# Value matmuls of B and C at full width with the denominators inside, and a limit on the projections per step

## The chip, the cores and the metric

The program runs on all 8 NeuronCores of one Trainium2 chip, one batch element each, with the same instructions on every core. The metric is the device time of the slowest core in microseconds. TensorE (PE in the profile) multiplies, ScalarE (ACT) computes exponentials and other functions, VectorE (DVE) combines and copies, GpSimd (POOL) and SyncE (SP) mainly start transfers. Each engine works through its own queue in order and waits on semaphores.

## The reference

Two layers; in each a mixer with three attentions in parallel and a SwiGLU network. D_MODEL is 1024, a core has 2048 frames. The part that the change touches are the attentions B and C, 8 heads of width 64 each:

```python
def forgetting_attention(q, k, v, f_logit):            # B: causal per frame
    ...
    sc = jnp.einsum('bqhd,bshd->bhqs', qb, k).astype(jnp.float32) * scale
    sc = sc + cq[..., :, None] - cum[:, :, None, :]
    sc = jnp.where(kpos[None, :] <= qpos[:, None], sc, NEG_INF)
    p = jax.nn.softmax(sc, axis=-1)
    return jnp.einsum('bhqs,bshd->bqhd', p.astype(v.dtype), v)

def chunked_relpos_attention(q, k, v, rel_table):      # C: own chunk and 8 before it
    ...
    sc = jnp.einsum('bqhd,bshd->bhqs', qc, kc).astype(jnp.float32) * scale + bias
    sc = jnp.where(valid[None, None, None, :], sc, NEG_INF)
    p = jax.nn.softmax(sc, axis=-1)
    return jnp.einsum('bhqs,bshd->bqhd', p.astype(vc.dtype), vc)
```

The kernel computes the softmax without a maximum: exponentials of the scores, their product with V, their sum over the keys (a product with ones), and a division at the end.

## The kernel before

`Prog` records operations per engine and derives the semaphore waits; each engine's queue is the order in which the Python code emits. Everything is feature-major: a tile of scores has 128 keys on the partitions and up to 512 queries (a group g, four of them) in the columns.

**Stages of a layer.** Attention A (31 steps), then four pairs of heads of B (36 steps each), four of C (18 each), then the merge of the branches, the output projection and the FFN. `seq` at the end of `build` lists the pairs; the two sets of buffers QK[s], VB[s] alternate.

**A step** (`run_steps`, L590) works on one pair of heads and one or two key tiles: the score matmuls of both heads into two banks, one exponential of ScalarE over both (PTF), then *filler*, and then, one step late, `emit_pv` (L558) with the value matmuls of the step before. Filler are the projections of the next pair, of which `pair_filler` (L767) hands out two matmuls at a time. `want` (L611) spreads them evenly over the steps: total is 96 per pair (106 in B of layer 0, with blocks of the conditioning). A projection unit has 8 matmuls of 512 columns (`proj_fm`) or 32 of 128 columns (`proj_v`) and ends with VectorE's evacuation of the one bank AJ; then a yield of 0 ends the filler of that step, and one of -1 (Q and K of a B pair) also skips the next step.

**Values and denominators.** `emit_pv` issues for each key tile and head a matmul with 64 columns of V, and one with 64 columns of ones, to partitions 0 to 63 or 64 to 127 of the banks `ob` (4 and 5 in turn) and DB (6). So both heads lie in one accumulator, and their denominators in another. `fin_pair` (L510) ends a group: Ln of the denominators in the same step, Exp of its negative in the next, the product by VectorE into OT in the one after; `run_pend` runs these stages.

Of the kernel before, what the change touches and what calls it, by code (L numbers as in the profile page):

```python
# [6 lines left out]
F32 = mybir.dt.float32  # L7
# [10 lines left out]
GS = 512  # L18
# [215 lines left out]
def build(order=None, nl=DEPTH):  # L234
# [33 lines left out]
    def sb(name, shape, dt):  # L268
        return nc.alloc_sbuf_tensor("sb_" + name, list(shape), dt)

    XR = sb("XT", [128, NG * 4096], F32)
    HT = sb("HT", [128, NCH, S], BF16)
    RR = sb("W", [128, 22528], BF16)
    NS = 6
    WS = sb("WS", [128, NS, 2048], BF16)
    RS = sb("RS", [128, 2, GS], F32)
    PT = sb("PT", [128, 8, GS], BF16)
    TMPF = sb("TMPF", [128, 3, GS], F32)
    RD = sb("RD", [128, 2, GS], F32)
# [216 lines left out]

    def proj_v(wv3, wb, t4, VB, vbufs, bi):
        for q in range(4):
            t = t4 * 4 + q
            pe_group([(PS[bi][:, q * 128:(q + 1) * 128], HT[:, kc, tl(t)], wv3[:, kc, :], kc == 0, kc == 7) for kc in range(8)],  # L500
                     [wb] + [ht[kc][t4] for kc in range(8)], [psb[bi]])
            if q < 3:
                yield 2
        copy("dve", VB[:, t4 * 512:(t4 + 1) * 512], PS[bi][:, :], [psb[bi]], [vbufs[t4]])

    def drain(gen):
        for _ in gen:
# [23 lines left out]
            tt(out, i0, i1, ALU.mult, [psb[ob], rdb[ri]], wr)  # L531
        return [st0, st1, st2]

    SETO = [0, 10240]
    QK = [[RR[:, o + i * 2048:o + (i + 1) * 2048] for i in range(4)] for o in SETO]
    VB = [RR[:, o + 8192:o + 10240] for o in SETO]
    qb = [[[Buf() for _ in range(NG)] for _ in range(4)] for _ in range(2)]
    augb = [[Buf() for _ in range(4)] for _ in range(2)]
    vbb = [[Buf() for _ in range(4)] for _ in range(2)]
    setbufs = [flat(qb[s]) + augb[s] + vbb[s] for s in range(2)]  # L540
    AO = 10240
    QA = RR[:, AO:AO + 8192].rearrange("p (c t) -> p c t", c=4)
    KA = RR[:, AO + 8192:AO + 10240]
    VA = RR[:, AO + 10240:AO + 12288]
# [7 lines left out]

    AJ = 7
    DB = 6
    HS = [slice(0, 64), slice(64, 128)]
    pipe = {"held": None, "pend": []}

    def emit_pv():  # L558
        if pipe["held"] is None:
            return  # L560
        st, pp, ptr = pipe["held"]
        pipe["held"] = None
        bi = st["ob"]
# [23 lines left out]
        while pipe["pend"]:  # L587
            run_pend()

    def run_steps(steps, filler, total):  # L590
        n = len(steps)
        given = 0
        cool = -1
        for i in range(n):
# [13 lines left out]
            if i == 0:  # L608
                emit_pv()
            if filler is not None and i > cool:  # L610
                want = total * (i + 1) / n  # L611
                while given < want:
                    c = next(filler, None)
                    if c is None:
                        filler = None
                        break
                    if c <= 0:
                        cool = i - c
                        break
                    given += c  # L620
# [161 lines left out]
    def pair_steps(l, is_b, s, p):  # L782
        k_out = 1 if is_b else 2
        steps = []
        for g in range(NG):
            ob = ob_alloc()
            started = []

            def fin(ob=ob, g=g):
                return fin_pair(ob, OT[k_out][:, p, sl(g)], [ot[k_out][p][g]])  # L790

            def add(kts, last=False):
                qk, bias, pv, pr = [], [], [], [onesbuf]
                qr = [cb] + ([qb[s][0][g], qb[s][1][g]] + augb[s] if is_b else [qb[s][0][g], biascb[s]])
                off = 0
                for j in kts:
# [13 lines left out]
                    else:  # L810
# [7 lines left out]
                            rows = HS[hh]  # L818
                            qk.append((hh, off, off + w, QK[s][2][rows, tl(j)], QK[s][0][rows, qs]))
                        qr.append(qb[s][2][j // 4])  # L820
                    pv.append((off, c0, c0 + w, VB[s][:, tl(j)], not started))
                    started.append(j)
                    pr.append(vbb[s][j // 4])
                    off += w
# [160 lines left out]
    for l in range(nl):  # L985
        a_rest(l)
        run_steps(a_steps(l), a_filler(l), 128)
        seq = [(True, p) for p in range(4)] + [(False, p) for p in range(4)]
        for i, (is_b, p) in enumerate(seq):
            run_steps(pair_steps(l, is_b, i % 2, p), pair_filler(l, i, seq) if i < 7 else None, 96 + (10 if l == 0 and i < 4 else 0))  # L990
        flush_pipe()
        wos = merge(l, x_d if l == 0 else xs_d)
        prev = None
# [151 lines left out]
```

How the kernel before makes its waits and increments, by code:

```python
        def run(e, engobj):  # L163
            for o in self.ops[e]:
                for ev in o.deps:
                    if ev.kind == "eng":
                        engobj.wait_ge(sems[ev.eng], ev.op.count)
                    else:
                        engobj.wait_ge(ev.sem, ev.value)
                inst = o.fn(engobj)
                if o.is_dma:
                    inst.then_inc(o.dma_sem, 16)
                elif o.needed:
                    inst.then_inc(sems[e], 1)
            if e == "sp":
                for b in final_waits:
                    ev = b.last_write
                    if ev is None:
                        continue
                    if ev.kind == "dma":
                        engobj.wait_ge(ev.sem, ev.value)
                    else:
                        engobj.wait_ge(sems[ev.eng], ev.op.count)
```

## Time and profile before

| what | value |
|---|---|
| median of 3 runs | 2815.0 us (2814.04 to 2816.72) |
| profiled execution | 2812.6 us, span 2810.8 us, 43124 instructions |
| cores in it | 2805.0 to 2810.8 us, granted TensorE clock 0.980 to 0.983 |
| TensorE busy | 2654.0 us (94%), 16192 matmuls |
| ScalarE, VectorE, GpSimd busy | 989.2 (35%), 983.3 (35%), 250.9 us (9%) |
| TensorE waits for ScalarE's probabilities (sb_PT) | 7.5 us, 25 times |
| TensorE waits for VectorE's sb_RD (A's denominators) | 43.8 us, 16 times |

In layer 0 of this execution the first pair of B begins at 252 us, C at 504.5, the merge at 663.2; in layer 1 at 1615, 1864.4 and 2023. In a timeline row the first number is the start in us from the start of the span and the second the duration of the row; "x8" stands for eight instructions of one form merged into one row; "128*64" is the number of rows and columns of the weights. A matmul's duration overlaps the next one's, so distances are taken from start to start. Score matmuls read sb_W,sb_W ("ps<-sb_W"), value matmuls sb_PT,sb_W, the ones sb_PT,sb_onesb, projections sb_HT and sb_WS.

### The profile page before, as it was taken

Reading aid. Unit: us, or ns where it says so; the run is one execution under the profiler, and the core shown is the slowest. Engines: PE = TensorE matmul, PEld = TensorE weight load, DVE = VectorE, ACT = ScalarE, POOL = GpSimd, SP = SyncE. Lnnn points to the kernel's source line nnn. Section 1 sums busy time; section 2 is a strip of 40 time slices with the busy share of each in tenths; the row PEclk is TensorE's granted clock in tenths of the full one; section 3 lists DMA queues with packets and bytes.
Section 4 is the critical chain, followed back from the end, with each engine's and each line's share of the span. In section 5 each row is a group of like instructions: output and inputs, shape, how many; then the busy total and the mean of one; then the engine's idle time right before and its main releaser. Section 6 shows DMA issues by size and latency. Waiting matters only on the chain.

```text
span 2810.8 us, 43124 instructions; the slowest of 8 cores (2805.0 to 2810.8 us)
## 1 busy us (share of the span) xinstructions
PE 2654.0 (94%) x16192; PEld 1203.2 (43%) x16192; DVE 983.3 (35%) x1471; ACT 989.2 (35%) x1334; POOL 250.9 (9%) x318
## 2 busy tenths in 40 slices
PE   1779999999999999999989799999999999999998
PEld 0323444554444444444433244445544444444443
DVE  1543222222444522223254522222244453232326
ACT  1355666544222421110144466654522234101012
POOL 2001000000000210000130010000000021000002
PEclk9889999999999999999999899999999999999999
DMA  9112222211223453343341010112122343222213
GB/s 214 16 27 41 47 47 35 53 30 24 35 34 48 118 92 68 53 77 59 68 136 23 9 18 17 20 20 55 18 34 40 51 113 53 38 38 38 45 31 120
DMA packets 68889, 147.83 MB, mean 53 GB/s; under 512 B 9504, under 2 KB 21920, under 8 KB 66640
## 3 DMA queue, kind: packets, MB, share of 16 engines
q0 software_dynamic: 55712, 99.66, 22.5%
q1 hardware_dynamic: 12976, 45.41, 4.8%
q8 instruction: 135, 2.21, 0.3%
q14 instruction: 66, 0.54, 0.1%
HBM read 227.53 MB, written 16.78 MB: 87 GB/s over the span
## 4 chain that ended last, share of the span: by engine, by line
PE 90%; DVE 3%; DMA 2%; ACT 2%; issue 2%; DVEq 0%; POOL 0%; POOLq 0%; ACTq 0%
PE ps L375 71%; PE ps L373 19%; DMA sb_WS<-wada 2%; ACT sb_PT L385 1%; ACT sb_HT L385 1%; DVE sb_XT L394 0%; DVE sb_RD L389 0%; DMA sb_WS<-win 0%; DVE sb_TMPF L394 0%; DVE sb_W L404 0%; DVE sb_XT L695 0%; DVE sb_W L398 0%; ACT sb_TMPF L385 0%; DMA sb_WS<-wfi 0%; DVE sb_XT L404 0%
## 5 line engine op out<-in xcount | busy, mean ns | idle before, releaser
L375 PE MATMUL ps<-sb_HT,sb_WS 128*128 128x512 bf16 (+1 forms) x5760 | 1342.9, 385 | 38.4 <-ACT sb_HT L385 22.4
L375 PEld LDWEIGHTS ps<-sb_HT,sb_WS 128*128 128x128 bf16 (+1 forms) x5760 | 556.4, 99 | 736.2 <-issue 108.3
L385 ACT ACTIVATE sb_PT<-ps 128x1024 bf16<-128x1024 f32 (+1 forms) x494 | 488.6, 989 | 430.8 <-PE ps L373 426.7
L385 ACT ACTIVATE sb_TMPF<-ps 128x512 f32<-128x512 f32 x388 | 231.3, 597 | 1141.6 <-PE ps L375 1141.4
L375 PE MATMUL ps<-sb_W,sb_WS 128*128 128x512 bf16 x1920 | 417.9, 379 | 1.2 <-DVE sb_W L389 1.1
L389 DVE TENSOR_TENSOR sb_W<-ps,sb_TMPF 128x512 bf16<-128x512 f32 x176 | 121.3, 691 | 484.5 <-PE ps L375 472.5
L375 PEld LDWEIGHTS ps<-sb_W,sb_WS 128*128 128x128 bf16 x1920 | 187.5, 98 | 227.2 <-issue 2.1
L404 DVE CAST sb_W<-ps 128x512 bf16<-128x512 f32 (+1 forms) x176 | 121.5, 690 | 408.5 <-PE ps L375 407.9
L373 PE MATMUL ps<-sb_W 128*128 128x512 bf16 (+7 forms) x1212 | 257.9, 340 | 0.0
L394 DVE SCALAR_TENSOR_TENSOR sb_XT<-ps,sb_modT,sb_XT 128x512 f32<-128x512 f32 x256 | 186.3, 748 | 154.2 <-PE ps L375 154.1
L373 PE MATMUL ps<-sb_PT,sb_onesb 128*64 128x512 bf16 (+3 forms) x1212 | 188.6, 336 | 44.4 <-DVE sb_RD L389 43.8
L373 PE MATMUL ps<-sb_PT,sb_W 128*64 128x512 bf16 (+3 forms) x1212 | 197.5, 352 | 8.9 <-ACT sb_PT L385 7.5
L375 PE MATMUL ps<-sb_XT,sb_WS 128*128 128x512 bf16 x768 | 197.1, 379 | 0.0
L389 DVE TENSOR_TENSOR sb_PT<-ps,sb_TMPF 128x512 f32<-128x512 f32 x128 | 88.5, 692 | 190.9 <-PE ps L375 184.7
L398 DVE TENSOR_SCALAR sb_W<-ps 128x512 bf16<-128x512 f32 (+1 forms) x128 | 88.0, 689 | 178.9 <-PE ps L375 178.1
L375 PE MATMUL ps<-sb_WS,sb_HT 128*128 128x128 bf16 x2304 | 144.0, 219 | 0.0
L375 PEld LDWEIGHTS ps<-sb_WS,sb_HT 128*128 128x128 bf16 x2304 | 132.8, 98 | 17.9 <-issue 8.3
L373 PEld LDWEIGHTS ps<-sb_W 128*128 128x128 bf16 (+1 forms) x1212 | 67.8, 95 | 158.5 <-issue 138.9
L389 DVE TENSOR_TENSOR sb_XT<-ps,sb_RD 128x512 bf16<-128x512 f32 x96 | 66.2, 689 | 182.6 <-ACT sb_RD L385 182.5
L373 PEld LDWEIGHTS ps<-sb_PT,sb_W 128*64 128x64 bf16 x1212 | 59.4, 107 | 164.6 <-issue 154.0
L375 PEld LDWEIGHTS ps<-sb_XT,sb_WS 128*128 128x128 bf16 x768 | 75.1, 98 | 90.6
L394 DVE SCALAR_TENSOR_TENSOR sb_TMPF<-sb_XT,sb_gsc,sb_RS 128x512 f32<-128x512 f32 x128 | 86.3, 745 | 47.5 <-ACT sb_RS L385 47.4
(53 smaller groups left out, 1187.7 us busy)
## 6 DMA issues: line engine op xcount, KB each, us to landing
sb_WS<-wada POOLq DMA_DIRECT2D x48, 512.0 KB, 9.3
sb_WS<-wfi POOLq DMA_DIRECT2D x44, 512.0 KB, 6.4
sb_WS<-wmg POOLq DMA_DIRECT2D x48, 384.0 KB, 5.7
sb_XT<-x SPq DMA_DIRECT2D x8, 2048.0 KB, 16.2
sb_WS<-win POOLq DMA_DIRECT2D x60, 256.0 KB, 4.3
sb_WS<-wfo POOLq DMA_DIRECT2D x24, 512.0 KB, 6.3
xs<-sb_XT SPq DMA_DIRECT2D x4, 2048.0 KB, 6.3
sb_XT<-xs SPq DMA_DIRECT2D x4, 2048.0 KB, 17.1
```

The lines of the kernel that those rows point to most:

```text
L373: r = e.matmul(o, lhsT=l, rhs=rr, start=st, stop=sp, skip_group_check=True)
L375: r = e.matmul(o, lhsT=l, rhs=rr, start=st, stop=sp)
L385: return P.op("act", lambda e, o=out, i=in_, f=func, kw=kw: e.activation(out=o, in_=i, func=f, **kw), reads=reads, writes=writes)
L389: return P.op(eng, lambda e, o=out, a=in0, b=in1, op=op: e.tensor_tensor(out=o, in0=a, in1=b, op=op), reads=reads, writes=writes)
L394: e.scalar_tensor_tensor(out=o, in0=a, scalar=s_, in1=b, op0=p0, op1=p1),
L398: return P.op(eng, lambda e, o=out, a=in0, s1=s1, p0=op0: e.tensor_scalar(out=o, in0=a, scalar1=s1, scalar2=None, op0=p0), reads=reads, wr ...
L404: return P.op(eng, lambda e, o=out, i=in_: e.tensor_copy(out=o, in_=i), reads=reads, writes=writes)
```

## The change

Each V tile gets 192 columns instead of 128: V of the even head, 64 ones, V of the odd head. A value matmul takes 128 of these as weights, so one matmul per key tile and head computes values and denominators, on opposite halves of one bank per head. Three banks (4, 6, 5) serve two accumulators per group in rotation. At a group's end `fin_two` first copies both banks to SBUF, then computes Ln per head across the halves, one Exp, and two half products. The ones are set once per set of buffers by GpSimd; the casts of V write in two pieces of 64 columns. `want` is two matmuls ahead of before and also limited per step: 6 (layer 0) or 4 (layer 1) in B, 8 in C, none in A. What is left is issued after the last step of a pair. A keeps `fin_pair`. The lines of after.py behind the change are two or more higher than before's.

```diff
-    RR = sb("W", [128, 22528], BF16)
+    RR = sb("W", [128, 23552], BF16)
+    OS = sb("OS", [128, 2, GS], F32)
...
-        copy("dve", VB[:, t4 * 512:(t4 + 1) * 512], PS[bi][:, :], [psb[bi]], [vbufs[t4]])
+        if len(VB.shape) == 2:
+            copy("dve", VB[:, t4 * 512:(t4 + 1) * 512], PS[bi][:, :], [psb[bi]], [vbufs[t4]])
+        else:
+            dst = VB[:, t4 * 4:t4 * 4 + 4, :].rearrange("p t (a c) -> p t a c", c=64)[:, :, 0:3:2, :]
+            copy("dve", dst, PS[bi][:, :].rearrange("p (t a c) -> p t a c", t=4, a=2), [psb[bi]], [vbufs[t4]])
...
+    def fin_two(ob, out, wr):
+        ri = next_rot("rd", 2)
+        def st0():
+            for hh in range(2):
+                copy("dve", OS[:, hh, :], PS[ob[hh]][:, :], [psb[ob[hh]]], [osb[hh]])
+        def st1():
+            for hh in range(2):
+                act(RD[HS[hh], ri, :], OS[HS[1 - hh], hh, :], AF.Ln, [osb[hh]], [rdb[ri]])
+            act(RD[:, ri, :], RD[:, ri, :], AF.Exp, [], [rdb[ri]], scale=-1.0)
+        def st2():
+            for hh in range(2):
+                tt(out[HS[hh], :], OS[HS[hh], hh, :], RD[HS[hh], ri, :], ALU.mult, [osb[hh], rdb[ri]], wr)
+        return [st0, st1, st2]
...
+    OB3 = [4, 6, 5]
...
+        if isinstance(bi, list):
+            for hh in range(2):
+                pe_group([(PS[bi[hh]][:, a:b], v[:, hh * 64:hh * 64 + 128],
+                           PTF[:, pp * 1024 + hh * GS + off:pp * 1024 + hh * GS + off + b - a], first, False, True)
+                          for (off, a, b, v, first) in st["pv"]], ptr + st["pr"], [psb[bi[hh]]])
+            if st["fin"] is not None:
+                f = st["fin"]()
+                f[0]()
+                pipe["pend"].append([f[1], f[2]])
+            return
...
-                want = total * (i + 1) / n
+                want = min(total * (i + 1) / n + 2, given + cap)
...
+            memset(VB[s][:, :, 64:128], 1.0, [vonb[s]] + vbb[s])
...
-            ob = ob_alloc()
+            ob = [OB3[next_rot("ob3", 3)], OB3[next_rot("ob3", 3)]]
...
-            run_steps(pair_steps(l, is_b, i % 2, p), pair_filler(l, i, seq) if i < 7 else None, 96 + (10 if l == 0 and i < 4 else 0))
+            run_steps(pair_steps(l, is_b, i % 2, p), pair_filler(l, i, seq) if i < 7 else None, 96 + (10 if l == 0 and i < 4 else 0), (6 if l == 0 else 4) if is_b else 8)
```

TensorE's queue in the first B pair of layer 1, from the first score matmuls (ps<-sb_W) of the third group, before:

```order
L373 MATMUL ps<-sb_W 128x512 x2
L373 MATMUL ps<-sb_PT,sb_W 64x256 x2
L373 MATMUL ps<-sb_PT,sb_onesb 64x256 x2
L373 MATMUL ps<-sb_W 128x512 x2
L375 MATMUL ps<-sb_HT,sb_WS 128x512 x8
L373 MATMUL ps<-sb_PT,sb_W 64x512 x2
L373 MATMUL ps<-sb_PT,sb_onesb 64x512 x2
L373 MATMUL ps<-sb_W 128x512 x2
L373 MATMUL ps<-sb_PT,sb_W 64x512 x2
L373 MATMUL ps<-sb_PT,sb_onesb 64x512 x2
```

and in the changed kernel:

```order
L375 MATMUL ps<-sb_W 128x512 x2
L375 MATMUL ps<-sb_PT,sb_W 128x256 x2
L375 MATMUL ps<-sb_W 128x512 x2
L375 MATMUL ps<-sb_PT,sb_W 128x512 x2
L375 MATMUL ps<-sb_W 128x512 x2
L377 MATMUL ps<-sb_HT,sb_WS 128x512 x4
L375 MATMUL ps<-sb_PT,sb_W 128x512 x2
L375 MATMUL ps<-sb_W 128x512 x2
L377 MATMUL ps<-sb_HT,sb_WS 128x512 x4
L375 MATMUL ps<-sb_PT,sb_W 128x512 x2
```

The matmuls with ones are gone, the value matmuls have 128 weight columns, and a unit of projections lies in two steps instead of one, followed by two steps without any (before too there were two without).

TensorE's queue at the end of the first C pair of layer 0, before:

```order
L373 MATMUL ps<-sb_W 128x512 x2
L375 MATMUL ps<-sb_WS,sb_HT 128x128 x32
L373 MATMUL ps<-sb_PT,sb_W 64x128 x2
L373 MATMUL ps<-sb_PT,sb_W 64x384 x2
L373 MATMUL ps<-sb_PT,sb_onesb 64x128 x2
L373 MATMUL ps<-sb_PT,sb_onesb 64x384 x2
L373 MATMUL ps<-sb_BIASC,sb_identb 128x256 x2
```

and in the changed kernel:

```order
L375 MATMUL ps<-sb_W 128x512 x2
L375 MATMUL ps<-sb_PT,sb_W 128x128
L375 MATMUL ps<-sb_PT,sb_W 128x384
L375 MATMUL ps<-sb_PT,sb_W 128x128
L375 MATMUL ps<-sb_PT,sb_W 128x384
L377 MATMUL ps<-sb_WS,sb_HT 128x128 x96
L375 MATMUL ps<-sb_BIASC,sb_identb 128x256 x2
```

Three units of V's projection (96 matmuls of 128 columns) now stand together between the last step of this pair and the first scores of the next (sb_BIASC is C's bias).

VectorE's queue in layer 0 while the second C pair runs, before (sb_XT<-ps,sb_RD is a group's final product; the casts and TENSOR_SCALAR to sb_W are evacuations of projections):

```order
L398 TENSOR_SCALAR sb_W<-ps 128x512
L389 TENSOR_TENSOR sb_XT<-ps,sb_RD 128x512
L398 TENSOR_SCALAR sb_W<-ps 128x512 x2
L389 TENSOR_TENSOR sb_XT<-ps,sb_RD 128x512
L398 TENSOR_SCALAR sb_W<-ps 128x512
L404 CAST sb_W<-ps 128x512 x2
```

and in the changed kernel:

```order
L400 TENSOR_SCALAR sb_W<-ps 128x512
L391 TENSOR_TENSOR sb_XT<-sb_OS,sb_RD 64x512 x2
L400 TENSOR_SCALAR sb_W<-ps 128x512
L406 COPY sb_OS<-ps 128x512 x2
L400 TENSOR_SCALAR sb_W<-ps 128x512
L391 TENSOR_TENSOR sb_XT<-sb_OS,sb_RD 64x512 x2
```

A group costs VectorE two copies and two half products instead of one product, and evacuations stand between them.

## Rows read from the trace of the kernel before

**Rows 1.** The page, section 4: shares by engine of the chain that ended last.
```profile
PE 90%; DVE 3%; DMA 2%; ACT 2%; issue 2%; DVEq 0%; POOL 0%; POOLq 0%; ACTq 0%
```

**Rows 2.** Windows: B, merge of layer 0; busy us (count) by engine, clock, DMA.
```profile
273.00:505.00 232.00, 230.56 (x1927) 104.37 (x1926) 57.02 (x90) 141.40 (x160) 14.30 (x24) 1.00 0.27 43
...
663.00:972.00 309.00, 309.00 (x1434) 139.99 (x1432) 149.03 (x216) 89.68 (x145) 31.70 (x39) 1.00 0.28 54
```

**Rows 3.** Groups by form: count, busy us, mean ns, idle before; three groups.
```profile
L385 ACT ACTIVATE sb_PT<-ps 128x1024 bf16<-128x1024 f32 x454 | 464.8, 1024 | 406.2 <-PE ps L373 402.5 <-ACT sb_PT L385 0.7
...
L385 ACT ACTIVATE sb_PT<-ps 128x512 bf16<-128x512 f32 x40 | 23.8, 596 | 24.5 <-PE ps L373 24.2
...
L407 POOL MEMSET sb_W<- 128x2048 bf16 x16 | 28.2, 1819 | 37.5 <-PE ps L373 37.5
```

**Rows 4.** Timeline, B of layer 0: start, us, engine, line, operation, idle before.
```profile
422.30 0.60 PE L373 MATMUL ps<-sb_W 128*128 128x512 bf16 x2
...
422.84 0.41 PE L373 MATMUL ps<-sb_PT,sb_W 128*64 128x512 bf16 x2
...
423.00 2.17 ACT L385 ACTIVATE sb_PT<-ps 128x1024 bf16<-128x1024 f32 x2 [1.79 <-PE ps L373]
423.08 0.38 PE L373 MATMUL ps<-sb_PT,sb_onesb 128*64 128x512 bf16 x2
...
423.39 0.60 PE L373 MATMUL ps<-sb_W 128*128 128x512 bf16 x2
...
424.17 0.41 PE L373 MATMUL ps<-sb_PT,sb_W 128*64 128x512 bf16 x2 [0.17 <-ACT sb_PT L385]
```

**Rows 5.** Timeline, B of layer 0, TensorE with eight projection matmuls.
```profile
419.49 0.60 PE L373 MATMUL ps<-sb_W 128*128 128x512 bf16 x2
...
419.93 1.89 PE L375 MATMUL ps<-sb_HT,sb_WS 128*128 128x512 bf16 x8
...
421.75 0.41 PE L373 MATMUL ps<-sb_PT,sb_W 128*64 128x512 bf16 x2
```

**Rows 6.** Chain of waits: the same place in successive B pairs, layers 0 and 1.
```profile
309.87 2.52 PE ps L373 x20
373.01 2.52 PE ps L373 x20
...
1646.23 2.52 PE ps L373 x20
...
1709.07 2.52 PE ps L373 x20
```

**Rows 7.** Timeline, C of layer 0, TensorE: scores, then projections or values.
```profile
590.51 0.39 PE L373 MATMUL ps<-sb_W 64*128 64x512 bf16 x2
...
590.83 1.96 PE L375 MATMUL ps<-sb_WS,sb_HT 128*128 128x128 bf16 x32
...
654.21 0.39 PE L373 MATMUL ps<-sb_W 64*128 64x512 bf16 x2
...
654.53 0.41 PE L373 MATMUL ps<-sb_PT,sb_W 128*64 128x128 bf16 x4
```

**Rows 8.** Timeline, last C pair of layer 0, ScalarE.
```profile
650.67 1.02 ACT L385 ACTIVATE sb_PT<-ps 128x1024 bf16<-128x1024 f32 x1
...
657.41 1.02 ACT L385 ACTIVATE sb_PT<-ps 128x1024 bf16<-128x1024 f32 x1
...
658.33 0.62 ACT L385 ACTIVATE sb_RD<-sb_RD 128x512 f32<-128x512 f32 x1
...
658.89 1.02 ACT L385 ACTIVATE sb_PT<-ps 128x1024 bf16<-128x1024 f32 x1
```

**Rows 9.** Timeline, B of layer 0: a unit of value projections and its cast.
```profile
425.17 1.95 PE L375 MATMUL ps<-sb_WS,sb_HT 128*128 128x128 bf16 x32
...
427.05 0.41 PE L373 MATMUL ps<-sb_PT,sb_W 128*64 128x512 bf16 x2
...
427.23 0.69 DVE L404 CAST sb_W<-ps 128x512 bf16<-128x512 f32 x1 [3.91 <-PE ps L375]
```

More of the change, by code:

```diff
@@ L325, in build @@
     rdb = [Buf() for _ in range(2)]
+    osb = [Buf() for _ in range(2)]
     a8b = Buf()
@@ L532, in fin_pair @@
         return [st0, st1, st2]
-    SETO = [0, 10240]
+    def fin_two(ob, out, wr):
[11 more added lines that the diff above has]
+        return [st0, st1, st2]
+    SETO = [0, 11264]
     QK = [[RR[:, o + i * 2048:o + (i + 1) * 2048] for i in range(4)] for o in SETO]
-    VB = [RR[:, o + 8192:o + 10240] for o in SETO]
+    VB = [RR[:, o + 8192:o + 11264].rearrange("p (t c) -> p t c", t=16) for o in SETO]
     qb = [[[Buf() for _ in range(NG)] for _ in range(4)] for _ in range(2)]
@@ L539, in build @@
     vbb = [[Buf() for _ in range(4)] for _ in range(2)]
-    setbufs = [flat(qb[s]) + augb[s] + vbb[s] for s in range(2)]
-    AO = 10240
+    vonb = [Buf() for _ in range(2)]
+    setbufs = [flat(qb[s]) + augb[s] + vbb[s] + [vonb[s]] for s in range(2)]
+    AO = 11264
     QA = RR[:, AO:AO + 8192].rearrange("p (c t) -> p c t", c=4)
@@ L588, in flush_pipe, with run_steps @@
             run_pend()
-    def run_steps(steps, filler, total):
+    def run_steps(steps, filler, total, cap=99):
         n = len(steps)
@@ L785, in pair_steps @@
         for g in range(NG):
-            ob = ob_alloc()
+            ob = [OB3[next_rot("ob3", 3)], OB3[next_rot("ob3", 3)]]
             started = []
             def fin(ob=ob, g=g):
-                return fin_pair(ob, OT[k_out][:, p, sl(g)], [ot[k_out][p][g]])
+                return fin_two(ob, OT[k_out][:, p, sl(g)], [ot[k_out][p][g]])
             def add(kts, last=False):
-                qk, bias, pv, pr = [], [], [], [onesbuf]
+                qk, bias, pv, pr = [], [], [], [vonb[s]]
                 qr = [cb] + ([qb[s][0][g], qb[s][1][g]] + augb[s] if is_b else [qb[s][0][g], biascb[s]])
@@ L820, in add @@
                         qr.append(qb[s][2][j // 4])
-                    pv.append((off, c0, c0 + w, VB[s][:, tl(j)], not started))
+                    pv.append((off, c0, c0 + w, VB[s][:, j, :], not started))
                     started.append(j)
@@ L987, in build @@
         run_steps(a_steps(l), a_filler(l), 128)
+        state["ob3"] = 0
         seq = [(True, p) for p in range(4)] + [(False, p) for p in range(4)]
         for i, (is_b, p) in enumerate(seq):
-            run_steps(pair_steps(l, is_b, i % 2, p), pair_filler(l, i, seq) if i < 7 else None, 96 + (10 if l == 0 and i < 4 else 0))
+            run_steps(pair_steps(l, is_b, i % 2, p), pair_filler(l, i, seq) if i < 7 else None, 96 + (10 if l == 0 and i < 4 else 0), (6 if l == 0 else 4) if is_b else 8)
         flush_pipe()
```

## The prediction

> **What bounds the kernel now.** I read the chain of waits first, then the stages, then single steps in the timeline. The chain is 90% TensorE [rows 1]: what counts is what TensorE's queue needs, plus the places where it waits. By stages [rows 2], the pairs of B of layer 0 (273 to 505 us) keep it busy over 99% at a granted clock of 1.00; ScalarE is at 61%, VectorE at a quarter. C and layer 1 have the same shape. The exponentials over a score tile count the steps [rows 3]: 454 + 40 = 494, of which A has 31 per layer, so B has 8 x 36 = 288 and C 8 x 18 = 144. A "busy" TensorE hides bubbles, though, since a matmul row is longer than its slot. So I take start-to-start distances. The merge is dense: 309.0 us for 1434 matmuls, 0.2155 us each [rows 2]; I call 0.216 one unit.
>
> A B step without projections [rows 4]: scores at 422.30, values at 422.84, ones at 423.08, next scores at 423.39. That is 1.09 us for four units (two score matmuls, two pairs of half-width ones side by side), 0.864. The excess sits at the borders: scores to values 0.54 instead of 0.43, values to ones 0.24 instead of 0.216, ones to scores 0.31 instead of 0.216. Scores to projections costs nothing (419.49 to 419.93, 0.44), but eight projection matmuls to values take 1.82 instead of 1.73 [rows 5]. So entering and leaving the half-width form costs about 0.10 each, and a step pays 0.225 with or without projections. Check: a B pair of layer 1 takes 62.8 us (1646.23 to 1709.07), one of layer 0 63.1 [rows 6]; the layer 1 pair has 240 units = 51.8 us, and 36 x 0.225 = 8.1, which leaves 2.9 for waits.
>
> The waits: after two steps without projections the value matmuls come 1.87 us after their scores (422.30 to 424.17) and not 1.63, 0.24 late, on the exponential that began at 423.00 [rows 4]. The chain scores, exponential, values is thus 0.70 + 1.02 + 0.15 us. Counted in the order: 8 such places in each of the first three B pairs of layer 1 and 5 in those of layer 0, 39 in all.
>
> **The change, part by part.**
>
> *Value matmuls.* Each key tile and head issued a half-width value and a half-width ones matmul, two heads side by side: two slots per key tile. Now it is one full-width matmul per head: also two slots. The arithmetic gains nothing; the borders go. B: 288 x 0.225 = 64.8 us. In C the scores themselves are in a form of 64 rows, which keeps its border: 590.51 to 590.83 is 0.32 for one unit, both to projections and to values (654.21 to 654.53) [rows 7]. A filled C pair pays 12 x 0.32 + 6 x 0.22 = 5.2 now and 18 x 0.10 = 1.8 afterwards: 3.4, times 6 = 20.2. The last C pair of a layer has no projections: 36 x 0.12 = 4.3. The 39 waits of 0.24 = 9.4 are replaced, not kept (next term). Removed: 98.7.
>
> Whether full-width weights hide behind a running matmul is the point where the Trainium skill and the rows part, in the two sentences that follow. "TensorE: Matmul & The Clock Gate", Part 3, The mechanism, says that a weight load overlaps running matmuls only when its row group differs, which for full-width matmuls would never be so. By that rule each new value matmul would pay its load as well; the merge, whose matmuls are all full-width, speaks against it [rows 2]: 140.0 us of weight loads lie inside 309.0 us of matmuls at 0.2155 each.
>
> *Steps with less cover.* TensorE's step falls to 0.864 without projections, but the chain of 1.87 stays. Two empty steps in a row: 1.30 against 1.87, 0.57 late; the new order has 1 such place in each of the first three B pairs of layer 0 and 8 in those of layer 1, 27 in all: 15.4 us. One empty step beside one with two matmuls: 1.73, 0.14 late, 26 places in layer 0: 3.6. I take 4 off, since some coincide with group ends.
>
> *Group ends.* There are 64, four in each of 16 pairs. Before, ScalarE did one Ln and one Exp in separate steps; now two Ln on 64 rows and one Exp in one block. Back to back in the last pair an exponential occupies 0.92, the Exp on the denominators 0.56, and I take 0.56 for each Ln [rows 8]. From the end of the scores of the group's second step: 0.27 + 0.92 + 3 x 0.56 + 1.02 + 0.15 = 4.04 until the next step's values may start. TensorE's own work there is eight units plus eight projection matmuls, 3.45. Late: 0.59. VectorE: two copies of the accumulators (0.69 each, as the cast of rows 9) free the banks. The second value matmul of the new group needs the first copy: the old group's last matmul of that bank streams 0.11, the copy starts 0.27 later and takes 0.69, 0.15 until TensorE: 1.22 us, against 0.86 of TensorE's work in between without projections (0.11 + 0.11 + 0.43 + 0.216): 0.36 late. This lies inside the window above, so I take 0.6 for both, 32 in B: 19.2. Bounds: 0 (always projections between) and 2.0 (copies behind an evacuation of 2 x 0.69). In C, steps carry eight matmuls or none: 0 to 0.5, taken 0.2, 24 groups of filled pairs: 4.8. VectorE's four operations of 0.69 instead of one add 132 us to 983; it has the room on average.
>
> *Pacing.* The limit per step, together with the skip after each unit, leaves work over: in the new order 96 and 80 matmuls of 128 columns stand at the end of 6 C pairs and of 3 B pairs of layer 1. They use one bank, so each unit of 32 waits for the cast of the one before: matmuls at 425.17, free at 426.96 (0.056 each), cast at 427.23 for 0.69 [rows 9], plus 0.15: 1.11 us. Two per place, 18: 20.0. Bounds 0.9 and 1.4 each. The projections themselves are the same in number.
>
> *The rest.* The last C pair of each layer is bound by ScalarE nearly as much as by TensorE: five steps take 6.7 us (650.67 to 657.41) [rows 8], and its five exponentials, two Ln and Exp come to 5 x 0.92 + 1.68 = 6.3 before dependences. I let the 4.3 removed there vanish; bounds 0 and 8. The fifth memset lies on GpSimd behind four of 1.82 [rows 3] and ahead of loads wanted much later: 0, at most 2. A has its matmuls and its waits in nearly the same places: 0, at most 3 either way. Merge and FFN don't change.
>
> Added: 15.4 + 3.6 - 4 + 19.2 + 4.8 + 20.0 + 4.3 = 63.3. Net -35.4. The profiled execution took 2812.6 us (span 2810.8), so 2777.2; the median of the runs is 2.4 above it: 2780.
>
> **Rivals.** (1) TensorE keeps its cover: group ends and empty steps cost nothing, only the drains: -98.7 + 20.0, 2736 us. For it: the fillers lie at half of the group ends, and TensorE runs dense. Against: the 0.24 is there already today. (2) ScalarE's chain rules: the waits are twice what I take (15.4 + 3.6 - 4 + 19.2 + 4.8 = 39 us more), 2819. For it: in layer 1 the steps' TensorE work falls to 47.5 us per pair (51.8 less the 20 units at the end) against 41.8 of ScalarE (32 x 1.02 + 4 x 0.60 [rows 3] + 4 x 1.68). Against: where a step has projections the chain has room. (3) Slower: VectorE as bottleneck of the bank rotation. With three banks for two accumulators, a copy that stands behind an evacuation (1.39) or behind the multiplications that wait for ScalarE's Exp stops TensorE at every group. With 1.1 more at 56 groups, 62 us more: 2842. It decides from 0.63 us more per group. For it: VectorE gets 2.8 us per group of which group 0 has only three steps. Against: the copies stand ahead of the multiplications of their group, and casts stand mostly two steps away. (4) The change doesn't do what it says: the border is not of the half-width form but of the wait for the probabilities; then 89 us don't go, 2869. Against it: ones to scores has no new wait for an exponential and pays the same 0.10. (5) Weight loads of 1088 full-width value matmuls come into the open, 0.098 each (140.0 / 1432) [rows 2]: +107, 2887. The sentence of the Trainium skill above would say so; the row says no.
>
> **How the numbers follow.** Forecast 0.58 (2760 to 2800), rival 1 0.17 (down to 2730), rival 2 0.15 (2800 to 2825, of which 0.08 still faster and 0.04 no change), rival 3 0.06, rival 4 0.03, rival 5 0.01. A measurement of this kernel can tell about 0.2%, 6 us. Faster 0.83, same 0.04, slower 0.13. Range: 2746 to 2815, half of rival 1 and the slow cases outside.
>
> **What would show it.** In the new profile: in B values start 0.43 after the scores and the next scores 0.43 after the values. B pairs near 59 us in layer 0 and near 62 in layer 1, of that about 2 in the drain; filled C pairs near 43.5, the last unchanged at 25. Waits of TensorE on ScalarE's probabilities rise from 7.5 us to some 40, and waits on VectorE appear once per group. Wrong if the borders of 0.10 are still there, if a wait on the accumulator copies exceeds 1 us on average, or if A, merge or FFN move by over 3 us.

## The result, and the profile after

The changed kernel took 2832.9 us (median of 5; 2829.3 to 2833.3 without disturbance) against 2816.7 for the kernel before: ratio of the undisturbed runs 1.0054, 95% interval 1.0036 to 1.0071. It is slower by half a per cent, where 2780 was forecast. The profiled execution took 2833.3 us, its span 2831.2.

The chain of waits of the changed kernel, by engine (share of the span):

```profile
PE 81%; ACT 6%; DVE 5%; issue 5%; DMA 2%; DVEq 0%; ACTq 0%; POOL 0%; POOLq 0%
```

TensorE's part fell from 90% to 81% [rows 1], ScalarE's and VectorE's rose from 5 to 11. That fits a shorter queue of TensorE with more waits in between; shares of a chain alone don't prove it, the rows below do. The windows of layer 0 of the changed kernel (us, then busy us by engine, granted clock, DMA) stand for B, three filled C pairs, and the last C pair:

```profile
254.00:509.00 255.00, 228.80 (x1760) 124.23 (x1790) 93.22 (x146) 166.02 (x193) 25.57 (x34) 0.97 0.29 45
509.00:643.00 134.00, 122.26 (x1078) 72.37 (x1088) 58.19 (x89) 75.62 (x91) 5.15 (x8) 1.00 0.21 43
643.00:675.00 32.00, 23.66 (x188) 12.46 (x187) 12.42 (x19) 25.05 (x31) 0.71 (x1) 0.90 0.09 14
```

B before kept TensorE busy 99% of its time at clock 1.00 [rows 2]; now it is 90%, at a mean of 0.97. What TensorE waits for in the whole changed kernel (total us, times, longest; L375 are scores and values, L377 projections; its waits for weight transfers and norms, such as 54.3 us for the conditioning's weights, were 50.5 before and are left out):

```profile
PE ps L375 <- DVE sb_RD L391: 43.1, 15, 4.6
PE ps L375 <- ACT sb_PT L387: 39.7, 60, 1.9
PE ps L377 <- DVE sb_W L406: 25.4, 36, 1.1
...
PE ps L377 <- DVE sb_modT L391: 9.5, 5, 2.9
...
PE ps L377 <- DVE sb_W L400: 6.4, 8, 1.0
PE ps L375 <- DVE sb_OS L406: 6.0, 6, 1.5
```

The first row is phase A, as before. The second was 7.5 us. The casts of projections (sb_W) and the add of the conditioning vector (sb_modT) were 1.4 us before and are 41 us together now. Now the timeline of B, layer 0, first at a place where TensorE doesn't wait, then at the end of a group:

```profile
410.05 0.59 PE L375 MATMUL ps<-sb_W 128*128 128x512 bf16 x2
410.48 0.59 PE L377 MATMUL ps<-sb_HT,sb_WS 128*128 128x512 bf16 x2
410.91 0.59 PE L375 MATMUL ps<-sb_PT,sb_W 128*128 128x512 bf16 x2
411.34 0.59 PE L375 MATMUL ps<-sb_W 128*128 128x512 bf16 x2
...
423.19 1.35 ACT L387 ACTIVATE sb_RD<-sb_OS 64x512 f32<-64x512 f32 x2
...
424.01 0.59 PE L377 MATMUL ps<-sb_HT,sb_WS 128*128 128x512 bf16 x2
...
424.63 0.63 ACT L387 ACTIVATE sb_RD<-sb_RD 128x512 f32<-128x512 f32 x1
425.17 1.92 ACT L387 ACTIVATE sb_PT<-ps 128x1024 bf16<-128x1024 f32 x2
425.36 1.48 DVE L391 TENSOR_TENSOR sb_XT<-sb_OS,sb_RD 64x512 bf16<-64x512 f32 x2 [2.34 <-ACT sb_RD L387]
426.32 0.59 PE L375 MATMUL ps<-sb_PT,sb_W 128*128 128x512 bf16 x2 [0.85 <-ACT sb_PT L387]
426.87 1.39 DVE L406 CAST sb_W<-ps 64x512 bf16<-64x512 f32 x2
428.41 1.46 PE L377 MATMUL ps<-sb_HT,sb_WS 128*128 128x512 bf16 x6 [1.07 <-DVE sb_W L406]
```

The first four rows: 0.43 from each to the next, so the borders of 0.10 around the half-width form [rows 4, 5] are gone, as forecast. The others show the group end: two Ln and an Exp occupy ScalarE from 423.19 to 425.17, and the values wait 0.85 for the exponential behind them. VectorE stands 2.34 us before the products, which need that Exp. The cast behind them had its data since the unit of projections ended at 424.60, comes after 1.48 us of products at 426.87, and bank 7 is free for projections only at 428.41: 1.07 more. The second wait was in no term of my sum.

Pair times, from first scores to the next pair's first scores (last C pair: to the merge's first matmul), profiled executions:

| us | before | changed | forecast |
|---|---|---|---|
| A, layers 0 / 1 | 109.4 / 106.4 | 109.4 / 109.3 | same |
| B layer 0, pairs 1 and 2 | 63.2 | 65.2 | 59 |
| B layer 1, pairs 0 to 2 | 62.9 | 62.2, 63.4, 63.2 | 62 |
| filled C pair | 44.4 | 45.0 | 43.5 |
| last C pair | 25.5 | 31.8 | 25.5 |

The fourth pair of B, whose projections are those of C, went from 62.6 to 61.4 in layer 0 and from 60.3 to 56.2 in layer 1. The table compares the slowest core of each execution. Most rows agree within 0.5 us on all eight cores; the second 65.2 is 63.7 on four of them, and the last C pair of layer 1 takes 31.8 to 33.8. A differs most: in layer 1 it takes 106.2 to 109.5 us on the cores of the kernel before and 106.2 to 109.3 on those of the changed one, so the 2.9 in the table is a difference between two cores and not the work of the change.

### The profile page after: what moved, and what is told of

It reads as the page before. It is cut to its first block, busy times and chain, and to the rows that moved or that the text cites. A ratio compares the mean times of both kernels' runs of the same rounds, so it can differ in the third digit from the quotient of the medians.

```text
span 2831.2 us, 41471 instructions; the slowest of 8 cores (2822.7 to 2831.2 us)
## 1 busy us (share of the span) xinstructions
PE 2592.6 (92%) x15104; PEld 1235.4 (44%) x15104; DVE 1109.2 (39%) x1663; ACT 1035.8 (37%) x1398; POOL 254.4 (9%) x322
## 4 chain that ended last, share of the span: by engine, by line
PE 81%; ACT 6%; DVE 5%; issue 5%; DMA 2%; DVEq 0%; ACTq 0%; POOL 0%; POOLq 0%
PE ps L377 69%; PE ps L375 13%; ACT sb_RD L387 2%; ACT sb_PT L387 2%; DMA sb_WS<-wada 2%; DVE sb_W L406 1%; DVE sb_OS L406 1%; ACT sb_HT L387 1%; DVE sb_XT L391 1%; DVE sb_XT L396 0%; DVE sb_TMPF L396 0%; DMA sb_WS<-win 0%; DVE sb_W L400 0%; DVE sb_RD L391 0%; DVE sb_XT L730 0%
## 5 line engine op out<-in xcount | busy, mean ns | idle before, releaser
L377 PE MATMUL ps<-sb_HT,sb_WS 128*128 128x512 bf16 (+1 forms) x5760 | 1353.3, 387 | 62.0 <-ACT sb_HT L387 22.4
L377 PEld LDWEIGHTS ps<-sb_HT,sb_WS 128*128 128x128 bf16 (+1 forms) x5760 | 558.4, 99 | 769.3 <-issue 144.5
L387 ACT ACTIVATE sb_PT<-ps 128x1024 bf16<-128x1024 f32 (+1 forms) x494 | 480.0, 986 | 401.6 <-PE ps L375 395.6
L377 PE MATMUL ps<-sb_W,sb_WS 128*128 128x512 bf16 x1920 | 418.0, 379 | 0.8 <-DVE sb_W L391 0.7
L375 PE MATMUL ps<-sb_PT,sb_W 128*128 128x512 bf16 (+4 forms) x1212 | 281.5, 340 | 46.9 <-ACT sb_PT L387 37.7
L377 PEld LDWEIGHTS ps<-sb_W,sb_WS 128*128 128x128 bf16 x1920 | 187.5, 98 | 226.8 <-issue 1.8
L375 PE MATMUL ps<-sb_W 128*128 128x512 bf16 (+7 forms) x1212 | 256.8, 340 | 0.0
L406 DVE CAST sb_W<-ps 128x512 bf16<-128x512 f32 (+1 forms) x176 | 121.5, 690 | 329.3 <-PE ps L377 311.5
L377 PE MATMUL ps<-sb_XT,sb_WS 128*128 128x512 bf16 x768 | 197.0, 379 | 0.0
L375 PEld LDWEIGHTS ps<-sb_PT,sb_W 128*128 128x128 bf16 (+1 forms) x1212 | 96.1, 99 | 175.3 <-issue 125.3
L377 PE MATMUL ps<-sb_WS,sb_HT 128*128 128x128 bf16 x2304 | 144.4, 219 | 18.3 <-DVE sb_W L406 17.7
L377 PEld LDWEIGHTS ps<-sb_WS,sb_HT 128*128 128x128 bf16 x2304 | 132.2, 98 | 36.4 <-issue 29.8
L391 DVE TENSOR_TENSOR sb_XT<-sb_OS,sb_RD 64x512 bf16<-64x512 f32 x128 | 87.9, 686 | 122.3 <-ACT sb_RD L387 114.8
L400 DVE TENSOR_SCALAR sb_W<-ps 128x512 bf16<-128x512 f32 (+1 forms) x128 | 87.9, 689 | 118.1 <-PE ps L377 109.4
L375 PEld LDWEIGHTS ps<-sb_W 128*128 128x128 bf16 (+1 forms) x1212 | 83.0, 96 | 103.5 <-issue 40.3
L377 PEld LDWEIGHTS ps<-sb_XT,sb_WS 128*128 128x128 bf16 x768 | 75.3, 98 | 91.2 <-issue 1.0
L406 DVE COPY sb_OS<-ps 128x512 f32<-128x512 f32 x128 | 82.3, 684 | 39.3 <-PE ps L375 39.0
```

The lines of the kernel that those rows point to most:

```text
L375: r = e.matmul(o, lhsT=l, rhs=rr, start=st, stop=sp, skip_group_check=True)
L377: r = e.matmul(o, lhsT=l, rhs=rr, start=st, stop=sp)
L387: return P.op("act", lambda e, o=out, i=in_, f=func, kw=kw: e.activation(out=o, in_=i, func=f, **kw), reads=reads, writes=writes)
L391: return P.op(eng, lambda e, o=out, a=in0, b=in1, op=op: e.tensor_tensor(out=o, in0=a, in1=b, op=op), reads=reads, writes=writes)
L400: return P.op(eng, lambda e, o=out, a=in0, s1=s1, p0=op0: e.tensor_scalar(out=o, in0=a, scalar1=s1, scalar2=None, op0=p0), reads=reads, wr ...
L406: return P.op(eng, lambda e, o=out, i=in_: e.tensor_copy(out=o, in_=i), reads=reads, writes=writes)
```

## The experiments

Theory P puts the loss on the pacing (the order in which projections are handed out), theory G on the group ends. First four kernels that part them. The cuts show the lines that matter; where a group end gets a fourth stage, `emit_pv` also hands all the later stages on.

```diff
 e1_wide_oldpace: the changed kernel, and
-                want = min(total * (i + 1) / n + 2, given + cap)
+                want = total * (i + 1) / n
 e2_pace_only: the kernel before with that line the other way round, and the caps
 e3_wide_noskip: the changed kernel, and
-                yield -1 if is_b else 0
+                yield 0
 e4_wide_fin3: the changed kernel, fin_two in four stages
+        def st2():
             act(RD[:, ri, :], RD[:, ri, :], AF.Exp, [], [rdb[ri]], scale=-1.0)
-        def st2():
+        def st3():
```

> The changed kernel with the old pacing: projections are handed out in proportion to the steps done, with no head start of two and no limit per step. Kernel before 2816.7, changed kernel 2832.9. Theory P (the new pacing spoils what the full-width matmuls gain: work left over at a pair's end and several steps without cover): 2790 to 2800, filled C pairs back at 43.5 us, B pairs of layer 0 at 61. Theory G (the gain is eaten at the group ends by the block of two Ln and one Exp on ScalarE, by VectorE's products and casts queued behind it, and by the half clock that TensorE's pauses bring on, whatever the pacing): 2825 to 2840.

Measured: 2811.5 us, ratio to before 0.9999 (0.9982 to 1.0017). Between both theories, in neither range. The full-width form with its group end alone gains nothing; pacing costs 21 us on top. B pairs of layer 0 take 61.8, C pairs 43.3, but the last C pair 32.8.

> The kernel before, half-width value matmuls and all, with only the new pacing (head start of two, limit of 6, 4 or 8 per step). Theory P: 2835 to 2850, by 18 drains of 1.1 us at the ends of 9 pairs and by new waits on the probabilities in steps without projections. Theory G: 2815 to 2825, since a half-width step of 1.09 us has room for the chain scores, exponential, values and the drains alone cost at most 20, against which the limit evens out the steps.

Measured: 2826.5 us, 1.0044 (1.0030 to 1.0059). Pacing alone costs 12. It is in the drains, the projections left over at a pair's end and issued together: C pairs take 46.2 instead of 44.4, B pairs of layer 1 65.0 instead of 62.9, while those of layer 0, which leave nothing over, fall by 0.1 to 0.9. Below theory P's range, above G's.

> The changed kernel with the skipped step in B removed: after a unit of projections whose result VectorE writes out, the next step takes projections again. Nothing is left over at a pair's end in B. Theory P: 2795 to 2810; the third B pair of layer 1 at 58 instead of 63. Theory G: 2825 to 2835, and a projection matmul then waits for its bank's cast in the next step.

Measured: 2759.6 us, 0.9808 (0.9794 to 0.9822), 35 us below what theory P hoped for at best: neither theory had this. Three quarters of the 73 us come from A, whose matmuls the change leaves as they were. It took 80.8 and 81.1 us instead of 109.4 and 109.3. The window of phase A, here 79 us of it, against the 106 us of the kernel before:

```profile
145.00:224.00 79.00, 73.50 (x450) 25.81 (x456) 47.20 (x73) 51.18 (x67) 2.71 (x4) 0.98 0.16 25
```

```profile
145.00:251.00 106.00, 84.48 (x448) 27.08 (x447) 48.06 (x72) 51.78 (x67) 1.98 (x3) 0.86 0.11 18
```

The same matmuls (450 and 448 records), in a quarter less time. A's ones matmuls need bank 6, which VectorE's operation into sb_RD has to free. A step without projections has nothing to put in between, and TensorE waits for it (21.5 us in layer 0 in both kernels, here 3.3). The mean granted clock of the kernel before is 0.86 there, here 0.98; how much of the gain is the clock's, no run parts. In B of layer 1 pairs fall from 63.3 to 57.1. In B of layer 0, pairs 1 and 2, nothing is gained (65.8 and 64.9).

> The changed kernel with the end of a group spread over one more step: both Ln in the second step of the new group, Exp in the third, the products on VectorE one step later. Order on TensorE unchanged. Theory P: within 5 us of 2833. Theory G: 2808 to 2822, since ScalarE's block shrinks from 1.9 to 1.3 us and VectorE's casts no longer stand behind products that wait for the Exp; waits of TensorE on probabilities fall from 40 us to 25 and on VectorE's casts from 25 to 12.

Measured: 2795.6 us, 0.9934 (0.9920 to 0.9948): 37 us off by moving the Exp and the two products of each group by one step. Theory G, and more than it expected (2808 to 2822). The waits on the probabilities fall from 39.7 to 25.2 us, as it said, those on the casts (L406) only from 25.4 to 19.1. From the chain of waits, the same piece of successive B pairs of layer 0, in the changed kernel and then in this one:

```profile
355.10 1.53 PE ps L375 x10
...
420.21 1.53 PE ps L375 x10
```

```profile
343.39 1.53 PE ps L375 x10
...
402.47 1.53 PE ps L375 x10
```

65.1 us against 59.1. Filled C pairs fall to 43.6. These are the numbers that the forecast had named, 59 and 43.5. The same place in its timeline:

```profile
405.45 1.35 ACT L387 ACTIVATE sb_RD<-sb_OS 64x512 f32<-64x512 f32 x2
406.83 1.02 ACT L387 ACTIVATE sb_PT<-ps 128x1024 bf16<-128x1024 f32 x1
406.96 1.39 DVE L406 CAST sb_W<-ps 64x512 bf16<-64x512 f32 x2 [1.68 <-PE ps L377]
407.75 0.62 ACT L387 ACTIVATE sb_RD<-sb_RD 128x512 f32<-128x512 f32 x1
408.00 0.59 PE L375 MATMUL ps<-sb_PT,sb_W 128*128 128x512 bf16 x2 [0.27 <-ACT sb_PT L387]
408.47 1.48 DVE L391 TENSOR_TENSOR sb_XT<-sb_OS,sb_RD 64x512 bf16<-64x512 f32 x2
```

An exponential now lies between Ln and Exp, the cast goes ahead of the products, and the values wait 0.27 instead of 0.85.

The second four: do the gains add up, does the skip matter without the wide form, is it VectorE's queue or ScalarE's block, and what does the clock cost?

```diff
 e5_noskip_fin3: both edits, of e3 and e4
 e6_before_noskip: the kernel before, and
-                yield -1 if is_b else 0
+                yield 0
 e7_products_late: as e4, but the Exp stays in st1, and st2 is empty
 e8_last_c_fill: the changed kernel, and a filler for the last C pair:
+        for _ in range(18):
+            pe_group([(PS[AJ][:, :], identb[:, :], HT[:, 0, sl(0)], True, True)] * 2, ...)
```

> The changed kernel with both edits: no skipped step after a Q or K unit, and the end of a group spread over one more step. Alone they gave 2759.6 and 2795.6 against 2832.9, that is 73 and 37 less. Theory S (two separate losses: the skipped steps cost A 28 us a layer and B of layer 1 6 us a pair; the group ends cost B of layer 0 6 us a pair and C 1.4): the gains add up but for the part in B that both touch, 2722 to 2735. Rival (both edits remove the same stalls, and one of them is enough): 2750 to 2760.

Measured: 2725.6 us, 0.9687 (0.9670 to 0.9704). 73 and 37 add up to 110, found 107: two separate losses, theory S.

> The kernel before, half-width value matmuls and all, with the skipped step in A and B removed. Theory S: the skip has nothing to do with the width of the value matmuls; phase A goes from 109.4 and 106.4 us to some 81, and the time to 2755 to 2770. Rival (in the kernel before the slot had its use, a cast needs the step, and the gain appears only with the wide form): 2800 to 2820.

Measured: 2766.0 us, 0.9830 (0.9814 to 0.9845). The skip is a loss of the kernel before too: A takes 83.9 and 85.3. So of e3's gain over the kernel before, only 6 us belong to the wide form, as theory S had it. The B pairs 1 and 2 of layer 0 lose 1.6 each by it (64.7), those of layer 1 gain 2.2 (60.6). Against this kernel e5 is 40 us faster; that is what the wide form, its limit and the spread group end are worth together.

> The changed kernel with only VectorE's two products of a group one step later; both Ln and the Exp stay together in the second step. The run with the Exp moved as well took 2795.6. Theory Q (the loss at the group ends is VectorE's queue: casts and the add of the conditioning vector stand behind products that wait for ScalarE's Exp): 2795 to 2805. Theory B (the loss is ScalarE's block of 1.9 us ahead of the next exponential): 2822 to 2833.

Measured: 2811.5 us, 0.9990 (0.9981 to 1.0000). 21 of e4's 37 us come from the products alone, 16 from the Exp: each theory holds a part. TensorE's waits in 255 to 500 us (B of layer 0) tell them apart; the changed kernel, then this one:

```profile
PE ps L377 <- DVE sb_modT L391: 9.5, 5, 2.9
PE ps L375 <- ACT sb_PT L387: 8.3, 12, 1.7
PE ps L377 <- DVE sb_W L406: 4.4, 7, 1.1
```

```profile
PE ps L375 <- ACT sb_PT L387: 11.8, 14, 1.7
PE ps L377 <- DVE sb_modT L391: 1.6, 2, 1.1
PE ps L377 <- DVE sb_W L400: 0.3, 1, 0.3
PE ps L377 <- DVE sb_W L406: 0.3, 1, 0.3
```

What TensorE waits for VectorE's queue goes from some 14 us to 2; the waits on the probabilities don't fall, they rise from 8.3 to 11.8. With the Exp moved as well (e4) they are 3.8.

> The changed kernel with two extra 128x512 matmuls per step, into an unused bank, in the last C pair of each layer, which has no projections; nothing reads them. They add 36 x 0.216 = 7.8 us of TensorE's work to a pair of 15.5 that takes some 28.5. Theory K (that pair is slow because TensorE pauses and is granted half its clock, 10 us per pair in two stretches): clock 1.00 there and the pair at 26 to 27, time 2826 to 2830. Theory L (ScalarE's chain sets the pair, the clock only follows): the pair stays at 28 to 29 or grows, time 2832 to 2840.

Measured: 2830.7 us, 1.0061 (1.0046 to 1.0076). My 28.5 ended at the pair's last step; to the merge's first matmul it is 31.8. The window of the last C pair with the fill:

```profile
643.00:675.00 32.00, 28.69 (x210) 13.84 (x208) 11.88 (x19) 24.82 (x31) 0.72 (x1) 1.00 0.10 13
```

Clock 1.00 instead of 0.90, and the pair at 33.3 instead of 31.8. Theory K's 26 to 27 is out: with the full clock alone the pair doesn't come back. The fill puts 7.8 us of work of its own into the pair, though, so that the clock costs nothing there is not shown. The whole time lies just above theory K's range and just below theory L's, and can't be told from the changed kernel's.

The third four take up the version at 2725.6 (e5).

```diff
 e9_last_c_narrow: in the last C pair
+            wide = is_b or p < 3
+            ob = [...] if wide else ob_alloc()
+                return (fin_two if wide else fin_pair)(
 e10_oldpace_best
-                want = min(total * (i + 1) / n + 2, given + cap)
+                want = total * (i + 1) / n
 e11_one_ln
-            for hh in range(2):
-                act(RD[HS[hh], ri, :], OS[HS[1 - hh], hh, :], AF.Ln, ...)
+            act(RD[:, ri, :], OS[:, 0, :], AF.Ln, osb, [rdb[ri]], bias=1.0, scale=0.0)
 e12_merge_bank: in merge
+        state["mgb"] = 3
```

> The version with no skipped step and the spread group end (2725.6), with the half-width value and ones matmuls back in the last C pair of each layer, which has no projections. That pair took 25.5 us in the kernel before, 31.8 in the changed kernel and 30.9 in this version. Theory U (in a pair without projections the wide form loses, since ScalarE does an Ln more per group and the copies hold the banks): the pair is back at 25.5 and the time at 2713 to 2717. Rival (the pair is slower for a reason outside its form, such as what the pair before it left queued): 30 or more, 2723 to 2727.

Measured: 2713.6 us, 0.9642 (0.9627 to 0.9657), as theory U said; the pair takes 26.4 and 25.3 instead of 30.9 and 30.8, and the C pair before it in layer 1, which shares a border with it, 1.1 more.

> The version at 2725.6 with the old pacing, in proportion and without a limit. Theory D (the new pacing leaves 96 matmuls over at the end of each filled C pair, which costs 1.7 us there and brings nothing): C pairs 41.9 instead of 43.6, B pairs within 1 us, time 2713 to 2719. Rival (the head start and the limit protect the group ends in B): B pairs 1 to 2 us longer, and the time 2722 to 2732.

Measured: 2741.6 us, 0.9740 (0.9727 to 0.9754). Outside both ranges, and by stages both halves can be seen: C pairs fell to 41.6, as expected, but B pairs of layer 0 rose from 58.9 to 65.0. There TensorE's waits on the accumulator copies (225 to 460 us) come to 10.8 us, against 2.3 with the new pacing (e9), and those on the casts of projections to 13.7 against 7.0; the granted clock is 1.00 in both. The head start and the limit do protect the group ends of B in layer 0, and do harm in C.

> The version at 2725.6 with one Ln over 128 rows in place of the two over 64 rows at each of the 64 group ends of B and C. It takes the logarithm of a constant, so the outputs of B and C are not divided by their sums. Theory A (ScalarE's extra Ln sets the last C pair): that pair goes from 30.9 us to 28.5, the time to 2719 or less. Rival B (the copies on VectorE and the banks set it): the pair stays within 0.5 us, and so does the time but for 1 or 2 us.

Measured: 2710.3 us, 0.9630 (0.9615 to 0.9644). Theory A, and beyond its 28.5: the last pair falls from 30.9 to 26.8, the whole by 15.4. B pairs gain 1.0 each on average, filled C pairs nothing. Part of the 4.1 can be the clock: the last pair of layer 0 has a stretch of 3.4 us at half the clock in e5 on every core, and here on one of eight. In the changed kernel the last C pair shows the block on ScalarE:

```profile
659.71 1.35 ACT L387 ACTIVATE sb_RD<-sb_OS 64x512 f32<-64x512 f32 x2
661.15 0.63 ACT L387 ACTIVATE sb_RD<-sb_RD 128x512 f32<-128x512 f32 x1
661.68 1.92 ACT L387 ACTIVATE sb_PT<-ps 128x1024 bf16<-128x1024 f32 x2
...
667.69 1.35 ACT L387 ACTIVATE sb_RD<-sb_OS 64x512 f32<-64x512 f32 x2
...
673.92 1.29 DVE L406 COPY sb_OS<-ps 128x512 f32<-128x512 f32 x2 [2.58 <-PE ps L375]
...
675.46 1.01 PE L377 MATMUL ps<-sb_HT,sb_WS 128*128 128x512 bf16 x2 [1.22 <-DVE sb_OS L406]
```

A group of five steps takes 7.98 us (659.71 to 667.69); before it took 6.74 for five steps [rows 8]. The two Ln take 1.44, 0.72 each from start to start, where I had 0.56.

> The version at 2725.6 with the rotation of the merge's banks begun at 3, so that its first gate matmul takes bank 7 instead of bank 4, which the last accumulator copy still has to free. If the 2.0 us between the last value matmul and the merge's first are this bank: 0.3 to 0.9 there, 2722 to 2724. If it is another wait: no change.

Measured: 2720.1 us, 0.9666 (0.9651 to 0.9680). The gap between the last value matmul and the merge falls from 2.03 to 0.43 in both layers. That explains 3.2 of 5.5 us; the rest is not traced, and the time is 2 below the range that was expected.

Two questions were left: do all the losses add up, and is a group end a matter of ScalarE's time or of the banks?

```diff
 e13_best: e5 with the edits of e9 and e12, and in C
+                want = total * (i + 1) / n   (B keeps the limit)
 e14_den_copy: e13, and
-                copy("dve", OS[:, hh, :], PS[ob[hh]][:, :], ...)
+                copy("dve", OS[HS[hh], 0, :], PS[ob[hh]][HS[hh], :], ...)
+                copy("dve", OS[HS[hh], 1, :], PS[ob[hh]][HS[1 - hh], :], ...)
     one Ln, one Exp and one product over 128 rows
```

> The version at 2725.6 (no skipped step, spread group end) with half-width matmuls in the last C pair, the old pacing in C alone, and the merge begun on bank 7. Theory (each loss stands by itself): 2725.6 less 12.0 for the last pairs, less 12 for six C pairs of 41.6 instead of 43.6, less 1 at the merge's start: 2698 to 2704. Rival (without the limit, C's group ends meet VectorE's casts, and the last C pair comes in with a queue): 2708 to 2716.

Measured: 2702.9 us, 0.9604 (0.9589 to 0.9619): the losses add up. It beats the changed kernel by 130 us and the kernel before, 2814.5 in this set of runs, by 112. Filled C pairs have lost their drains; the same piece of its chain in two of them, 41.6 us apart:

```profile
510.38 1.83 PE ps L377 x8
...
551.95 1.83 PE ps L377 x8
```

> As the run beside it, but VectorE copies numerators and denominators apart (four copies of 64 rows instead of two of 128), so that ScalarE does one Ln and one Exp over 128 rows and VectorE one product. One Ln less gave 15 us at a cost of nothing. Theory V (it is ScalarE's time at the group end that counts): 5 to 12 us faster than the run beside it. Theory W (the banks count as well, since they come free after four copies of 0.65 us instead of two): 0 to 25 us slower.

Measured: 2742.5 us, 0.9744 (0.9729 to 0.9760), 39.6 slower than e13; theory W, and beyond its range. VectorE's rows at one group end in B of layer 0:

```profile
419.28 2.85 DVE L406 COPY sb_OS<-ps 64x512 f32<-64x512 f32 x4 [2.85 <-PE ps L375]
422.16 0.69 DVE L400 TENSOR_SCALAR sb_W<-ps 128x512 bf16<-128x512 f32 x1
424.38 0.69 DVE L391 TENSOR_TENSOR sb_XT<-sb_OS,sb_RD 128x512 bf16<-128x512 f32 x1 [1.53 <-ACT sb_RD L387]
```

Four copies of half the rows occupy VectorE for 2.85 us, two of all rows 1.29 (the last C pair above), so what stands behind them comes 1.5 us later; B pairs of layer 0 rise to 62 and C pairs to 43.7. The 15 us of the Ln can't be bought this way.

## Why the prediction was wrong

**Borders (98.7 removed).** Right. The rows at 0.43 show it, and rival 4 (another cause of the border) and rival 5 (weight loads in the open) are out: 410.05 to 411.34 holds six full-width matmuls, 0.215 each. As to the sentence of the Trainium skill ("TensorE: Matmul & The Clock Gate", Part 3, The mechanism) that a weight load overlaps running matmuls only when its row group differs: the trace does not agree with it here. In C the borders can only be judged with the drains away: e13's filled pair is 2.8 below the kernel before, where the terms for borders and group ends gave 2.6.

**Steps with less cover (15.4 in layer 1) and drains (20).** Right in size. Without skip and drain a B pair of layer 1 falls by 6.2 us (e3); the terms gave 4.6 and 2.2, and no run parts the two. In C the old pacing takes 2.0 a pair off (e5 to e13); the drain's term was 2.2.

**Group ends (24).** This is the step that failed. "Late: 0.59" counted ScalarE's block, "0.36 late" the first copy. It left out what is queued on VectorE behind the products, which wait for the Exp: the casts, for which bank 7 and so the next projections wait, and the conditioning add. Spreading the end gives back 37 us, more than the whole term: 21 in B of layer 0, 2 in B of layer 1, 9 in filled C pairs, 2 in the last, the rest outside these; 21 of the 37 hang on the products, 16 on the Exp. Rival 3 named the products that wait for the Exp, but only with the copies behind them, and I set it aside with "the copies stand ahead of the multiplications of their group, and casts stand mostly two steps away". The rows at 424.01 to 428.41 show a cast that does not: its unit ends in the group's second step. Rival 3 was nearest in time (2842) and in mechanism, only that the copies themselves were seldom the wait (sb_OS some 8 us in all).

**The last C pair (4.3 removed, 4.3 added).** Wrong in size: 6.3 more than before in each layer, 12.6 together. With the 4.3 removed, 16.9 were added, twice my bound of 8. Two terms are behind it: an Ln of 0.72 more per group in a pair that ScalarE bounds (e11: 4.1 us less with one Ln), and 1.6 at the merge's first bank (e12), which I had not looked at, since the copies now stand between the last values and the merge.

**A (0, at most 3).** Right as far as it can be told: the cores of one execution differ by 3 us in layer 1, before and after alike, as said under the pair times.

**TensorE's clock.** The prediction counted at 1.00 throughout. The changed kernel is granted half of it (1.2 instead of 2.4 GHz) in stretches of 3.4 to 6.8 us in B of layer 0 and in the last C pair. One begins on core 2 at 388.8, while TensorE waits 2.85 us for the conditioning add (387.26 to 390.12). Core 0 waits the same 2.85 at this place and keeps its clock, so the wait alone does not decide it. The price can be read from the changed kernel by itself. The same piece of pair 2 on core 0, which runs 3.7 us ahead, and on core 2:

```profile
382.30:395.30 13.00, 8.47 (x58) 4.01 (x55) 5.74 (x10) 9.04 (x12) 1.44 (x2) 1.00 0.97 144
```

```profile
386.00:399.00 13.00, 9.46 (x50) 3.96 (x48) 5.74 (x10) 8.26 (x13) 1.44 (x2) 0.74 1.08 174
```

Core 0 did this pair in 63.7 us, core 2 in 65.2: 1.5 us for a stretch of 6.8. Core 2 has three such stretches in B of layer 0 (3.4, 6.8 and 6.8 us) and none in B of layer 1: by my estimate some 4 us, a small part of the miss. In e4 and e7 no core has one in B of layer 0. So of the 21 us that e4 gives back there some 4 are the clock's, which came back when the waits went; TensorE's waits themselves fall from 23.4 to 9.1 us (255 to 500 us).

Added up against the terms of the sum (2777.2, the profiled execution took 2833.3, 56 more): B 32, filled C pairs 5, last C pairs 13, A 3 (the cores compared), the rest 3. Of the 32 in B, 23 are the group ends as spread by e4. The rest is partly my own: the terms give 57 us for a B pair of layer 0, and I wrote "near 59" beside them, 8 us in four pairs that the sum did not have. That e4 then took 59 is luck: no term gives it.

## What to carry to other kernels

An operation that waits for another engine holds up everything behind it in its queue. When a change adds one, list what the next two steps put behind it and who waits for that, not only how long it takes; here an Exp and its products, moved by one step, were worth 37 us. Put the parts of an epilogue (copy, Ln, Exp, product) into separate steps, so that each engine has its regular work in between. A gain per step holds only where a step has cover: in stages without filler check the other engine's sum, and keep the old form there. Before a difference of 3 us in one stage is put down to a change, look at that stage on every core of both executions. And test the scheduler's rules on the old kernel too: the skipped step cost the kernel before 47 us in phase A, which the change left alone.

## What the runs showed of the hardware

Rows cost nothing: one copy by VectorE of 64 rows by 512 lasts 0.69 us (e14), one of 128 rows also 0.69 (e13), and one Ln by ScalarE from SBUF 0.63 with 64 rows (e13) or 128 (e14). What differs is the distance to the next instruction: 0.72 between the four half copies of e14, 0.61 between the two whole ones of e13; 0.72 from an Ln of 64 rows to the next operation into the same sb_RD (659.71 to 661.15 for two), 0.52 from an Ln of 128 rows to an exponential into another tile, from a bank (601.71 to 602.23 in e9) or from SBUF (602.86 to 603.38 in e11). Whether the rows, the start partition or the shared tile make it longer, no run parts. The cores of one execution part in the granted clock on equal work: in pair 2 of B of layer 0 four of them had the stretch of 6.8 us and four did not.
